# A two-layer diffusion-transformer step on one core: weights behind a norm split ahead of it, and two row blocks' high parts made by VectorE

## What is computed

```
def layer(x, cond, p, ctx):
    mod = (silu(cond) @ p['w_mod'] + p['b_mod'])
    shift1, scale1, gate1, shift2, scale2, gate2 = split(mod, 6)
    h = rms_norm(x, p['norm1_g']) * (1 + scale1) + shift1
    out, ctx_out = mixer(h, p, ctx)
    x = x + gate1 * out
    h2 = rms_norm(x, p['norm2_g']) * (1 + scale2) + shift2
    x = x + gate2 * (square(relu(h2 @ p['w_ff1'])) @ p['w_ff2'])
```

## Time and profile before

| what | value |
|---|---|
| median of 3 runs | 2052.89 us (2051.81 to 2057.48) |
| the profiled execution's own time | 2052.7 us |
| its span, first to last instruction | 2050.9 us |
| PE busy | 1979.8 us, 97% of the span |
| DVE busy | 1207.2 us, 59% |
| ACT busy | 943.7 us, 46% |
| POOL busy | 276.6 us, 13% |
| mean granted TensorE clock | 0.993 of full speed |

### The profile page before, as it was taken

How to read it: one execution, slowest core, us unless ns; L and a number is a source line. 1 busy time by engine, 2 the same in 40 slices (tenths; PEclk the granted TensorE clock), 3 DMA queues, 4 the chain that set the end, 5 groups by cost and what they waited for, 6 DMA issues and landing times.

```text
span 2050.9 us, 34098 instructions
## 1 busy us (share of the span) xinstructions
PE 1979.8 (97%) x13988; PEld 1811.0 (88%) x13988; DVE 1207.2 (59%) x2087; ACT 943.7 (46%) x1740; POOL 276.6 (13%) x225
## 2 busy tenths in 40 slices
PE   6999999999999999999999999999999999999997
PEld 3995688999888999999989856889999899999997
DVE  4245688756468273746563366887564755646464
ACT  5535544534366162524455355454442743535262
POOL 1000000232012130403100000003220202121210
PEclk9999999999999999999999999999999999999999
DMA  9210001344523424242532100113453222213131
GB/s 369 74 52 12 1 27 53 122 161 135 185 78 112 144 88 147 75 139 89 169 110 67 39 11 1 39 58 129 151 168 132 62 83 66 91 62 103 62 96 59
DMA packets 53035, 195.92 MB, mean 96 GB/s; under 512 B 6032, under 2 KB 8144, under 8 KB 52112
## 3 DMA queue, kind: packets, MB, share of 16 engines
q1 hardware_dynamic: 49408, 174.61, 25.7%
q0 software_dynamic: 3472, 19.14, 2.6%
HBM read 187.79 MB, written 5.93 MB: 94 GB/s over the span
## 4 chain that ended last, share of the span: by engine, by line
PE 86%; DVE 7%; ACT 3%; DMA 2%; issue 2%; SPq 0%; ACTq 0%; DVEq 0%
PE ps L747 40%; PE ps L899 23%; PE ps L919 3%; PE ps L814 2%; PE ps L1065 2%; PE ps L928 2%; PE ps L765 2%; PE ps L852 2%; PE ps L1041 2%; PE ps L1095 2%; PE ps L1070 1%; DVE w_lo_parts L1693 1%; DMA w_raw<-in_stream 1%; ACT scratch L1513 1%; DVE scratch L2101 1%
## 5 line engine op out<-in xcount | busy, mean ns | idle before, releaser
L1693 DVE TENSOR_TENSOR w_lo_parts<-w_raw,w_hi_parts 128x512 fp32r<-128x512 f32 x546 | 403.8, 759 | 240.2 <-ACT w_hi_parts L1279 142.2
L1279 ACT CAST w_hi_parts<-w_raw 128x512 fp32r<-128x512 f32 x300 | 174.5, 619 | 455.4 <-PE ps L747 414.3
L747 PE MATMUL ps<-hid_hi_parts,w_hi_parts 128*128 128x320 f32 x1216 | 280.3, 312 | 0.9 <-issue 0.6
L747 PE MATMUL ps<-hid_hi_parts,w_lo_parts 128*128 128x320 f32 x1216 | 277.0, 309 | 0.0
L747 PE MATMUL ps<-hid_lo_parts,w_hi_parts 128*128 128x320 f32 x1216 | 277.0, 309 | 0.0
L1891 DVE SCALAR_TENSOR_TENSOR x<-ps,modulation,x 128x128 f32<-128x128 f32 (+2 forms) x216 | 81.7, 434 | 317.6 <-PE ps L747 317.6
L747 PEld LDWEIGHTS ps<-hid_hi_parts,w_hi_parts 128*128 128x128 f32 x1216 | 201.9, 188 | 23.9 <-issue 21.8
L1283 ACT CAST w_hi_parts<-w_raw 128x512 fp32r<-128x512 f32 x246 | 148.5, 621 | 136.6 <-PE ps L747 60.7
L747 PEld LDWEIGHTS ps<-hid_hi_parts,w_lo_parts 128*128 128x128 f32 x1216 | 203.3, 188 | 0.0
L747 PEld LDWEIGHTS ps<-hid_lo_parts,w_hi_parts 128*128 128x128 f32 x1216 | 203.3, 188 | 0.0
L899 PE MATMUL ps<-h_hi_parts,w_hi_parts 128*128 128x320 f32 x548 | 170.0, 310 | 0.0
(11 more groups left out here) (334 smaller groups left out, 4036.6 us busy)
## 6 DMA issues: line engine op xcount, KB each, us to landing
w_raw<-in_stream SPq DMA_DIRECT2D x312, 512.0 KB, 3.8
scratch<-in_first SPq DMA_DIRECT2D x10, 512.0 KB, 14.0
small_weights<-in_small POOLq DMA_DIRECT2D x2, 2048.0 KB, 10.7
h_scratch<-in_first SPq DMA_DIRECT2D x6, 512.0 KB, 17.0
x<-in_xT POOLq DMA_DIRECT2D x2, 1280.0 KB, 11.3
x<-in_xT POOLq DMA_DIRECT2D x8, 320.0 KB, 4.4
x_kept<-x POOLq DMA_DIRECT2D x8, 320.0 KB, 2.5
x<-x_kept POOLq DMA_DIRECT2D x8, 320.0 KB, 4.4
```

Of the source, the lines that this page charges most:

```text
L747: ins = mm(out[:, h, :], weight(w, s, k), a[:, k, h * HALF:(h + 1) * HALF], start=(first and n == 0), stop=(last and n == 2))
L1279: copy(place(wh, r), raw_half(s, n)).then_inc(w_hi, 1)
L1693: return tt(dst, full, hi.bitcast(F32), ALU.subtract)
```

## The change

1. Weight tiles 0 and 1 behind each of the three boundaries, and tile 0 at the start, no longer take places in the ring of split weights. They get places of their own, laid over buffers that are idle there (small_weights, low_rank_latents, gate_prefix_sums, gla_r). They are split before the norm: in `last_two` instead of in `norm`, on ACT and on DVE. The ring holds the other tiles, so that tiles 2 and 3 behind a norm find their places free earlier; their `split_next` stands ahead of the wait for the product where it stood behind it (tile 2).
2. The high parts of row blocks 6 and 7 of the first half are made by DVE (`tensor_scalar`, new line 1892) and no longer by ACT.
3. NORM_LAG becomes (2, 2), and DVE's `norm` runs as one loop over both halves, with low parts three blocks behind (`ahead = 3`), but the last three low parts of the first half together ahead of the wait for the second factor.
4. ACT's table load for Ln in the norm moves from behind block 4 to behind block 2.
5. In the last norm DVE's `last_add` moves from ahead of block 4 to ahead of block 1. In `first_norm` entries 2 and 3 of the weights are subtracted inside the loop.

More of the change, by code:

```diff
@@ L320, in build @@
         mix_full_a = nc.alloc_sbuf_tensor_at("mix_diff_a", [P, 3, KT // 2, HALF], F32, offset=at[0])
+        early_w_ff = nc.alloc_sbuf_tensor_at("early_weights", [P, 8, KT // 2, P], F32R, offset=at[0])
         sm = sb("small_weights", [P, SM_N])
@@ L593, in block_source, with early_place @@
                     raw_half(s, 1), raw_half(s + 1, 1))[n]
+        def early_place(low, r):
+            s, n, _ = ENTRIES[r]
+            if s % PER >= FF0:
+                return early_w_ff[:, 4 * (s % PER - FF0) + 2 * low + n, :, :]
+            if s % PER == 0:
+                return early_w_a[:, 2 * low + n, :, :]
+            return (early_w_b_lo if low else early_w_b_hi)[:, n, :, :]
         def place(w, r):
[L597 removed]
+            if r not in RING_AT:
+                return early_place(int(w is wl), r)
+            c = RING_AT[r]
+            return w[:, c % 4 // 2, 4 * (c % 2):4 * (c % 2) + 4, :]
         def weight(w, s, k):
@@ L614, in by_scale, with hi_made @@
             return p == 1 and k % 2 == 0
+        def by_vector(p, k):
+            return p == 0 and k in HI_BY_VECTOR
+        def hi_made(n, p, k):
+            made = [not by_vector(a, b) for a in range(2) for b in range(KT)]
+            return n * sum(made) + sum(made[:p * KT + k + 1])
         def unit_bank(u):
@@ L1817, in half_sum, with last_two @@
                 tt(M[:, 0, cols], M[:, 0, cols], M[:, KT - 2, cols], ALU.add).then_inc(sums, 1)
-            def last_two(b, o, gate):
+            def last_two(b, o, i, gate):
                 for j in range(2):
@@ L1852, in norm_low, with norm @@
                 ins.then_inc(h_ready, 1)
-            def norm(n, layer, b, o, i, gate, ahead=2):
+            def norm(n, layer, b, o, i, gate, ahead=3):
                 dve.wait_ge(mod_read, 6 * layer + (2 if n == 0 else 5))
-                for p in range(2):
-                    dve.wait_ge(rstd, e.at(rstd, 2 * b + p + 1))
-                    for k in range(KT + ahead):
-                        if k < KT:
-                            hat(n, p, k).then_inc(xhat, 1)
-                        if k >= ahead:
-                            norm_low(n, layer, p, k - ahead)
-                        if p == 0 and k == 1:
-                            half_sum(b, 1)
-                        if p == 0 and k == 2:
-                            split_next(i)
-                            modulation(i)
-                        if p == 0 and k == 3:
-                            last_add(o + 1, gate)
-                        if p == 0 and k == KT - 1:
-                            split_next(i + 1)
-                            modulation(i + 1)
+                for j in range(2 * KT + ahead):
[11 more added lines that the diff above has]
+                        last_add(o + 1, gate)
+                    if j == KT - 1:
+                        modulation(i + 1)
             def first_norm(ahead=2):
@@ L1882, in first_norm @@
                             norm_low(0, 0, p, k - ahead)
+                        if p == 0 and k in (1, 2):
+                            low_entry(k + 1)
             def mix_low(k):
@@ L1905, in _ @@
                 hat(0, 1, k).then_inc(first_hat, 1)
-            for r in range(4):
+            for r in range(2):
                 low_entry(r)
@@ L2187, in _ @@
                     modulation(OUT0 + q)
-                last_two(0, O_OUT + OUT_TILES - 2, 2)
+                last_two(0, O_OUT + OUT_TILES - 2, OUT0 + OUT_TILES - 2, 2)
                 norm(1, e.layer, 0, O_OUT + OUT_TILES - 2, OUT0 + OUT_TILES - 2, 2)
@@ L2229, in _ @@
                         modulation(i + KT + q)
-                last_two(1, PAIRS - 2, 5)
+                last_two(1, PAIRS - 2, PER - 2, 5)
                 if e.layer + 1 < DEPTH:
```

27 lines of the change are left out of this document (21 added, 6 removed).

## The result

The changed kernel takes 2043.66 us (median of 4 runs, 2041.57 to 2043.92); the kernel before, beside it, 2054.55 (4 runs, 2051.81 to 2057.48). The ratio is 0.9946, 95% interval 0.993 to 0.9961: faster by 0.5%. The forecast was 2040.5. The profiled execution took 2043.45 us, its span is 2041.4 (before 2052.7 and 2050.9), so the two executions differ by 9.3 us (their spans by 9.5) where the sum of the steps said 12.3.

The account below looks back on a forecast made before the run. About 7 us of each of three boundaries counted as lost, with PE waiting on DVE and ACT. Boundaries 11.0 + start 0.2 + end 1.1 = 12.3 off 2052.7 gave 2040.4, stated as 2040.5; range 2036.5 to 2046.

Parts of the forecast that it names:

- (a): At a boundary, four weight subtractions move from the norm into DVE's waits and cost nothing; without that cover, up to 1.2 us.
- (b): Boundary's first blocks: PE's 1.25 us delay goes; it idles some 0.9 before low part 1 and 0.4 before low part 2.
- (c): Blocks 6 and 7 wholly on DVE: TENSOR_SCALAR 0.39 us plus 0.04 wait for its result; the 0.71 stall goes.
- (d): Second factor at 1608.45 instead of 1609.35; second half's first hat 2.26 us earlier, DVE and factor arriving together.
- (e): Second half of the norm, left as it was: 9.2 us from first hat to last low part.
- (f): End of a boundary: with lag 2, four half steps (1.76 us) follow the last block; 3.7 us gained per boundary.
- (g): Tile 2: weights ready 0.9 us before PE wants them, bank freed 0.4 before; no wait, little cover.
- Start: Kernel's start: reordered weight subtractions, two TENSOR_SCALARs on DVE and the shorter lag net 0.2 us (0 to 0.6).
- End: Kernel's end: the last add starts at 2038.56 instead of 2039.67, and the chain to the store gains 1.1 us.
- The clock: Rival: PE's new short waits bring one low-clock stretch per boundary, costing 4.2 us in all, so 2044.8; chance 0.20.
- Less gain: Rival: DVE or ACT gives less than summed (slow TENSOR_SCALAR, late bank or weights), so 2047.5; chance 0.10.
- The slower rival: Stalls keep PE at 1.2 GHz through the boundaries, making it the bound: +5.1 us each, 2067; chance 0.03.

Follow-up runs that it names:

- Experiment 7: Changed kernel with ACT's casts of tile 2's weights again behind the wait for product 0: 2046.48 us, ratio 0.9958.
- Experiment 3: Changed kernel with high parts 6 and 7 made by ACT again instead of DVE: 2045.81 us, ratio 0.9965.
- Experiment 2: Changed kernel with NORM_LAG back at (6, 5): 2045.03 us, ratio 0.995.
- Experiment 4: Kernel before the change with only NORM_LAG set to (2, 2): 2069.31 us, ratio 1.007.
- experiment 6: Changed kernel with NORM_LAG (1, 1) in place of (2, 2): 2043.09 us, ratio 0.9942.
- experiment 1: Changed kernel run again, nothing altered: 2042.6 us, ratio 0.9948.
- experiment 10: Changed kernel run once more, nothing altered, as reference for two variants on one chip: 2042.85 us, ratio 0.9945.
- experiment 8: Changed kernel with DVE's last add of the last norm back ahead of hat 4 instead of hat 1: 2041.25 us, one run.
- Experiment 5: Changed kernel with ACT instead of POOL making full_h of group 2 in the feed-forward, half of POOL's work there: 2040.0 us, ratio 0.9933.
- Experiment 9: Changed kernel with POOL's feed-forward block sums cut to 128 of 512 columns, so not usable: 2038.51 us, ratio 0.9922.

## Why the prediction was right, and where it fell short

The forecast lay 3.2 us below the first median and 2.4 below that of all 15 runs, inside the range; faster was right. No run takes back the early places of tiles 0 and 1, the moved table load or the new loop on DVE by itself, so what is said of (a), and of `ahead = 3`, rests on the timelines. Step by step:

- **(a)** Right. The four subtractions stand in DVE's waits for PE, and the first half step has no gap. Experiment 7 shows that for tile 2 the place matters as much.
- **(b)** Right: waits of 0.79 and 0.22 against 0.9 and 0.4.
- **(c)** Right: TENSOR_SCALAR 0.38 against 0.39, and 0.04 for its own result. (Rows 7 are not all there is: DVE has two more of 128x640 with 494 ns, L1921, and POOL has some of 128x320; the 0.39 doesn't hang on them.) Experiment 3 prices the part at 1.4 a boundary.
- **(d)** Right to 0.05: first hat to first hat of the second half is 9.58 (I had 1598.89 to 1608.5). DVE and factor arrive together.
- **(e)** Right: 9.2 from the first hat to the end of the last low part.
- **(f)** Right: 18.2 us. Experiment 2 prices the lag at 1.1 a boundary; three half steps of 0.44 would be 1.3, and I did not follow the difference. Experiment 4 shows that this part exists only on top of the others.
- **(g)** Right, and close: weights ready 0.9 and bank 0.4 ahead of tile 2. Experiment 7 shows that moving the casts is what keeps the weights on time, and experiment 6 uses up the cover of the bank.
- **Start**: 1.1 against 0.2. Of it 0.7 was there before the norm began (DVE's hats started at 31.43 us and not 32.15). In experiments 1 and 10 the hats start at 32.03 and 32.12, and there equal matmuls near 52 us lie 0.1 earlier and 0.2 later than in the kernel before. So the 1.1 was luck, and of the 0.2 these traces show nothing. **End**: 1.1, confirmed by experiment 8.

**What failed is the sum**, "11.0 for three": it took every microsecond won at tile 2 for won at the end. I had followed PE to tile 2 and stopped. Behind the first boundary stands a second consumer of h that isn't PE: POOL and DVE need 24 us from the last low part of h to the first product by sevens (606.68 to 631.03 before, 605.29 to 629.43 after), and PE already waited 0.37 for them before the change. That chain moves with the last low part of h, by 2.3 us (steps (b) to (d)), and not with PE, by 3.7. What PE wins beyond the chain must come back as a wait, and does. Counted from the boundary's start, PE comes there 3.9 us sooner (42.36 to 38.48: 3.6 of the boundary, 0.3 of the load), and the last weights of the chain are there 2.5 sooner (42.73 to 40.26); the wait grows by the difference, 1.78 - 0.37 = 1.4. The lag of 1 in experiment 6 gives nothing there for the same reason. Experiments 5 and 9 shorten that very chain (to 39.2 and to 38.3 or less), and the wait shrinks.

The chain isn't rigid, though. With long lags (experiment 2) it takes 39.3 and not 40.3, so the short lag itself makes it 0.9 longer, and the split of tile 2 ahead of its old place makes POOL's part 11.30 long where it is 8.94 in experiment 7 (DVE starts later there, so that the whole is 40.5 all the same). The same chain stands behind the third boundary, but there nothing is waited for, before or after (idle 0.00 at 1655.11 and 1646.77): layer 1 has six tiles ahead of its first product by sevens and layer 0 four (`first_seven`). Whether more such tiles in layer 0 would keep the gain was not tried.

So the sum should have read 3.7 + 3.7 + 2.3 + 1.3 = 11.0, that is 2041.7 for the profiled execution; against the median of all runs of before it gives 2042.9, and 2042.85 was measured. This sum was made after the result, and that it fits to 0.1 is luck: it still holds 0.2 for the start, and what lies outside the boundaries moves by more. The rest of the 9.3 in the first pair of traces is chance: attention and one load against it, the start for it.

**The rivals.** The clock did not fall: 1.00 at every boundary of every changed version, with waits of 0.2 to 0.8 us. "TensorE: Matmul & The Clock Gate" of the Trainium skill (A second HAM failure mode) tells of micro-idles that made the clock of another kernel oscillate; it gives no length for them, and those here did not do it. The low clock came with longer waits, though not with each: two of three of 1.76 us before, those of 1.92 and 1.38 ahead of the stretches in attention (166.66 in the first trace, 339.01 in that of experiment 1), and that of 3.27 in experiment 4. The new wait at the first product by sevens is of that kind: behind 1.78 and 1.86 us the clock stayed at 1.00 (the changed kernel, experiment 10), behind 1.90 in experiment 8 it was 0.61 and 0.54 over the next four us. The drain of "ScalarE: Activation LUTs" of the Trainium skill (What ACT_TABLE_LOAD costs) isn't in the trace after either (Exp starts 0.01 behind the load), and 3.6 a boundary and not 2.3 was won. (The 2.3 was also wrongly priced: a drain with each switch would have stood in the factor's chain before the change too, and so hardly in the difference.) "Less gain" had the right kind of cause at the wrong place. The slower rival, a low clock that keeps itself low, was not seen: in experiment 4 the clock was at 0.50 from 1618 to 1624, behind a stall for weights, and at 0.92 in the two us after that.

## What to carry to other kernels

When a stall is removed, follow the result to each of its consumers, on every engine, up to the next place where PE already waits: what arrives there sooner than the slowest chain moves is given back. Here that was 1.4 of 3.9 us. In these runs a shorter lag between two interleaved products paid only if their weights were ready before the first of them started; price such parts as a set, since alone one of them may cost more than the set gains. An order in which a small reduction stands behind a stalled matmul turns a wait of 3 us into one of 6 on the engine that needs its result.

## What the runs showed of the hardware

- **DVE and POOL slow each other down** where both work from SBUF at once. Two low parts of weights take DVE 1.28 us alone, 3.49 beside POOL's block sums and 1.82 beside short ones; two differences of 128x1280 take 5.08 and 3.42 (2.89 with POOL idle, at 616.91 in the kernel before), and POOL's first block sum 2.30 beside DVE and 1.38 to 1.51 in four other traces. It was there before the change too: the same differences took 5.09. The Trainium skill says so in "SBUF — State Buffer" (SBUF: two separate sides): the shared port pair is held for a whole instruction, by a DVE operation with two SBUF inputs too, and the other side waits. The trace agrees that both sides get slower and that shorter sums help; no run shows the lock itself. POOL's full_h, which has one input, goes at 1.41 us apiece after the change (11.30 for 8) and at 1.13 before (9.00). Experiment 7 puts only the split of tile 2 back, so that DVE's subtractions no longer lie beside the first of them, and has 8.94 again.
- **TENSOR_SCALAR of 128x320 from float32 to the rounded form** takes 0.38 us, the SCALAR_TENSOR_TENSOR beside it 0.55.
- **Stretches of low clock in attention** move from run to run in unchanged code, and cost 1.5 and 3.0 us in the two traces read above. The slowest runs of experiment 1 also have the lowest mean clock (0.993 and 0.992 at 2048.14 and 2046.41 us, 0.995 or 0.996 in the others), so such stretches are likely a good part of the scatter; only the profiled executions have a trace to show it.
